# Delta rule with unscaled q and k: norms moved into gate tables, u and the output norm; triangle blocks loaded in pieces

## What is computed

```
q = jnp.repeat(l2_norm(q), rep, axis=2) * DN_HEAD_DIM ** -0.5     # l2_norm(x) = x * rsqrt(sum(x*x) + 1e-6)
k = jnp.repeat(l2_norm(k), rep, axis=2)
g = -exp(a_log) * softplus(a + dt_bias);  beta = sigmoid(b);  gc = cumsum(g) in the chunk
m = where(strict, beta * (k k^T) * decay, 0) + eye                 # decay = exp(gc_i - gc_j)
u0, w = triangular_solve(m, [v * beta, k * beta * exp(gc)])
u = u0 - w @ state;  o = q_dec @ state + (q k^T * decay) @ u;  state = cd * state + k_dec^T @ u
o = rms_norm(o, out_g)
```

## Time and profile before

| | |
|---|---|
| median of 3 runs | 3026.83 us (3018.61 to 3031.2) |
| the profiled execution, and its span | 3026.03 us, 3024.1 us |
| PE busy | 2846.4 us (94%) |
| DVE, ACT, POOL busy | 1903.4 us (63%), 1408.8 us (47%), 362.9 us (12%) |
| mean granted PE clock | 0.975 |

### The profile page before, as it was taken

One profiled execution on the slowest core, in us unless ns is written; L12 is line 12 of the kernel. 1 busy time (PEld: TensorE's weight loads), 2 busy tenths in 40 slices (PEclk: granted clock), 3 DMA queues, 4 the chain that ended last, 5 costly groups with the idle time before them and its releaser, 6 DMA issues.

```text
span 3024.1 us, 46453 instructions
## 1 busy us (share of the span) xinstructions
PE 2846.4 (94%) x19394; PEld 2681.0 (89%) x19394; DVE 1903.4 (63%) x2801; ACT 1408.8 (47%) x2399; POOL 362.9 (12%) x338
## 2 busy tenths in 40 slices
PE   6999998798999999999989999998999999999996
PEld 6999998687888999999988999998887899988775
DVE  5546647642333544656456855776888888878886
ACT  5346544355555433443335204433555555545554
POOL 0000010011112000002200002222122111112210
PEclk9999999899999999999999999999999999999998
DMA  4444435422232554444434458998999988889984
GB/s 185 169 157 145 171 103 178 150 98 73 78 100 94 204 181 169 167 168 158 157 127 156 152 203 312 371 362 325 366 361 363 357 326 317 324 333 345 357 338 142
DMA packets 112048, 668.47 MB, mean 221 GB/s; under 512 B 28336, under 2 KB 28552, under 8 KB 33920
## 3 DMA queue, kind: packets, MB, share of 16 engines
q1 hardware_dynamic: 86976, 496.93, 45.4%
q0 software_dynamic: 23712, 164.11, 14.8%
q10 hardware_dynamic: 1152, 4.47, 0.4%
HBM read 651.54 MB, written 13.30 MB: 220 GB/s over the span
## 4 chain that ended last, share of the span: by engine, by line
PE 66%; DVE 13%; DMA 10%; ACT 7%; issue 2%; SPq 0%; POOL 0%; DVEq 0%; ACTq 0%
PE PS L1001 66%; DMA raw<-in_pv 8%; DVE WL L1626 5%; DVE m L1617 3%; ACT WH L2304 3%; ACT m L2289 2%; DMA m<-in_pv,keep 1%; DVE m L2129 1%; ACT L2289 1%; DVE m L1817 1%; DMA raw<-in_w_kv 1%; DVE m L1814 0%; ACT m L2290 0%; PE PS L1004 0%; DVE m_896r L2222 0%
## 5 line engine op out<-in xcount | busy, mean ns | idle before, releaser
L1626 DVE TENSOR_TENSOR WL<-raw,WH 128x1024 fp32r<-128x1024 f32 x804 | 985.5, 1233 | 672.8 <-ACT WH L2304 671.9
L2304 ACT CAST WH<-raw 128x1024 fp32r<-128x1024 f32 x804 | 837.3, 1046 | 571.2 <-PE PS L1001 371.6
L1001 PE MATMUL PS<-m_4096r,WH 128*128 128x256 f32 x5184 | 997.9, 293 | 31.1 <-DVE m_4096r L1617 11.5
L1001 PEld LDWEIGHTS PS<-m_4096r,WH 128*128 128x128 f32 x5184 | 827.1, 196 | 54.7 <-issue 13.2
L1001 PE MATMUL PS<-m_4096r,WL 128*128 128x256 f32 x2592 | 743.5, 287 | 0.0
L1001 PE MATMUL PS<-m_8192r,WH 128*128 128x256 f32 (+1 forms) x2560 | 561.1, 313 | 16.7 <-issue 11.1
L1001 PE MATMUL PS<-WH,m_896r 128*128 128x512 f32 x1536 | 524.1, 394 | 24.6 <-DVE m_896r L2222 24.5
L1001 PEld LDWEIGHTS PS<-m_4096r,WL 128*128 128x128 f32 x2592 | 507.1, 196 | 0.0
L1001 PEld LDWEIGHTS PS<-m_8192r,WH 128*128 128x128 f32 x2560 | 398.6, 194 | 19.6 <-issue 11.7
L1001 PE MATMUL PS<-m_8192r,WL 128*128 128x192 f32 (+1 forms) x1792 | 405.1, 273 | 0.0
L1001 PE MATMUL PS<-WL,m_896r 128*128 128x512 f32 x1024 | 401.5, 392 | 0.0
(11 more groups left out here) (228 smaller groups left out, 1869.7 us busy)
## 6 DMA issues: line engine op xcount, KB each, us to landing
raw<-in_pu SPq DMA_DIRECT2D x128, 1024.0 KB, 6.9
raw<-in_pv SPq DMA_DIRECT2D x128, 1024.0 KB, 8.7
raw<-in_w_qkv SPq DMA_DIRECT2D x48, 1024.0 KB, 4.8
raw<-in_w_o SPq DMA_DIRECT2D x48, 1024.0 KB, 4.8
raw<-in_w SPq DMA_DIRECT2D x40, 1024.0 KB, 4.8
raw<-in_w_z SPq DMA_DIRECT2D x32, 1024.0 KB, 4.9
raw<-in_w_kv SPq DMA_DIRECT2D x16, 1024.0 KB, 4.8
raw<-in_w_q SPq DMA_DIRECT2D x16, 1024.0 KB, 4.8
```

The lines of the kernel that those rows point to most:

```text
L1001: return e.matmul(o, l, x, start=start, stop=stop)
L1626: tt(WL[:, k, :], raw[:, n % NRAW, h * 1024:h * 1024 + 1024], WH[:, k, :].bitcast(F), ALU.subtract).then_inc(S["lo"], 1)
L2304: e.copy(WH[:, k, :], raw[:, n % NRAW, h * 1024:h * 1024 + 1024]).then_inc(S["hi"], 1)
```

## The change

Q and k stay as they come from the Silu. Of their norms, `RNK` = 1/|k| for 24 columns goes into two gate tables (beta for the inverse's table `BEN`, and the table `BX` that scales k into kb), into the rows of the stored k products (`iv_product`, now on DVE, line 1788 of the new kernel), and into u (`dn_u_`, ACT with a column of RNK as scale). The norm of q goes into the eps of the output norm, `EPSQ`, for which DVE gets an instruction of its own (`ysc`) between PE's sums and the Sqrt. The 12 `rn_spread` steps are gone, with the three parts after each. `iv_turn` now waits for DVE's `rn`. After `iv_out` stand 28 parts where 16 stood. The loads are in pieces with semaphores of their own: the block between (`im`) is stored and loaded after the third scaling; U is stored before the turning copy and T after it; POOL issues the loads of the first two groups. SP loads T and the block between of group g+2 once `X` of group g is done, and gates and U once `o3` is.

```
-        for n in range(12):
-            self.do("rn_spread", n)
-            yield
         st["n"] = True
...
         self.do("iv_out")
-        for g in range(2):
-            self.do("dn_load", g)
-        yield 16
+        yield 28
...
         self.do("dn_uc", g)
+        if g < 10:
+            self.do("dn_load_t", g + 2)
...
         self.do("dn_y", g)
         if g < 10:
-            self.do("dn_load", g + 2)
+            self.do("dn_load_u", g + 2)
...  SyncE
+            def dn_load_t(g):
+                s.wait_ge(*at(f"dn_pe{g % 2}", dn_at(DN_PE, g - 2, "X")))
+                for c in range(2):
+                    load_t(e, g, c)
+                    load_bt(e, g, c)
+            def dn_load_u(g):
+                s.wait_ge(*at(f"dn_pe{g % 2}", dn_at(DN_PE, g - 2, "o3")))
+                load_gates(e, g)
+                for c in range(2):
+                    load_u(e, g, c)
...  TensorE
             def iv_turn():
-                p.wait_ge(*at("keep", 1))
-                p.wait_ge(*at("rn_root", 1))
-                tr(PS[0:48, 2, 0:128], KEEP[:, 192:240])
-                tr(PS[0:48, 2, 128:256], KEEP[:, 48:96]).then_inc(S["iv_turn"], 1)
+                p.wait_ge(*at("rn", 1))
+                tr(PS[0:48, 2, 0:128], GC)
+                tr(PS[0:48, 2, 128:256], BEN).then_inc(S["iv_turn"], 1)
...  dn_in
-                p.wait_ge(*at(f"ld_dn{g % 2}", 176 * (g // 2 + 1)))
+                p.wait_ge(*at(t_sem(g), 96 * max(g // 2, 1)))
...  dn_uc
+                p.wait_ge(*at(u_sem(g), 80 * max(g // 2, 1)))
...  VectorE
             def rn_root():
                 v.wait_ge(*at("rn_root", 1))
-                v.step(recip(RN, RN))
+                ts(EPSQ, PS[:, 2, 0:24], 1e-6, 128e-6, ALU.add, ALU.mult)
+                v.step(recip(RNK, RNK))
                 v.own()
-                one(RN[:, 0:24], RN[:, 0:24], 128.0 ** -0.5, ALU.mult).then_inc(S["rn"], 1)
+                v.step(tt(by_head(BEN), by_head(BE), per_group(RNK), ALU.mult))
+                v.own()
+                tt(by_head(BX), by_head(BX), per_group(RNK), ALU.mult).then_inc(S["rn"], 1)
-            def rn_spread(n):
-                c = (n + 6) % 12
-                q = QK[:, c * 512:c * 512 + 512]
-                v.wait_ge(*at("rn_spread", n + 1))
-                v.wait_ge(*at("silu", 24))
-                tt(q, q, PS[:, 2 + (n + 1) % 6, :], ALU.mult).then_inc(S["qkn"], 1)
+            def iv_product(c):
+                v.wait_ge(*at("iv_product", c + 1))
+                for h in range(2):
+                    rows = slice(64 * h, 64 * h + 64)
+                    o = IV_STG[rows, 256 * c:256 * c + 256].rearrange("p (i k) -> p i k", i=4)
+                    scale = RNK[rows, 4 * c:4 * c + 4].unsqueeze(2).broadcast_to([64, 4, 64])
+                    tt(o, c4(PS[rows, 2 + (c + 1) % 6, :])[:, :, rows], scale, ALU.mult).then_inc(S["iv_kept"], 1)
             def dn_yss(g):
+                need_p(g, "yss")
+                mark(g, "ysc", stt(rr.rearrange("p (h t) -> p h t", h=2),
+                                   PS[:, dn_bank(g)[0], 0:4].rearrange("p (h t) -> p h t", h=2), 1.0 / 128, eps, ALU.mult,
+                                   ALU.add))
                 need_a(g, "yrt")
...  ScalarE
             def dn_u_(g, n):
-                mark(g, f"ut{n}", e.copy(dn_u(g)[b:b + 64, :], PS[b:b + 64, dn_bank(g)[0], 0:256]))
+                mark(g, f"ut{n}", act(dn_u(g)[b:b + 64, :], PS[b:b + 64, dn_bank(g)[0], 0:256], ACT.Copy,
+                                      scale=RNK[b:b + 64, 2 * g + t:2 * g + t + 1]))
             def dn_yss(g):
-                need_p(g, "yss")
-                mark(g, "yrt", act(dn_s(g)[:, 0:4], PS[:, dn_bank(g)[0], 0:4], ACT.Sqrt, scale=1.0 / 128, bias=C("eps6")))
+                need_v(g, "ysc")
+                mark(g, "yrt", act(dn_s(g)[:, 0:4], dn_s(g)[:, 0:4], ACT.Sqrt))
...  GpSimd
+            def iv_save(name, x):
+                for h in range(2):
+                    e.dma_start(by_chunk(scratch[name], h), x[48 * h:48 * h + 48, :]).then_inc(S[f"st_{name}"], 16)
+            def iv_scale(b):
+                if b < 2:
+                    return
+                g_.wait_ge(*at("iv_between", 1))
+                iv_save("im", IV_E[:, 2048:3072])
+                g_.wait_ge(*at("st_im", 32))
+                g_.wait_ge(*at("iv_zero", 6))
+                for g in range(2):
+                    for c in range(2):
+                        load_bt(e, g, c)
             def iv_out():
+                g_.wait_ge(*at("iv_inverse", 1))
+                iv_save("iu", IV_U)
                 g_.wait_ge(*at("iv_done", 1))
+                iv_save("it", IV_T)
+                g_.wait_ge(*at("st_iu", 32))
+                for g in range(2):
+                    for c in range(2):
+                        load_u(e, g, c)
+                    g_.wait_ge(*at("st_it", 32))
+                    for c in range(2):
+                        load_t(e, g, c)
+                    load_gates(e, g)
```

More of the change, by code:

```diff
@@ L122 @@
 DN_PE = ("X", "A", "C", "UC", "W", "u0", "s0", "u1", "o1", "s1", "u2", "o2", "s2", "u3", "o3", "yss", "ybc")
[L123 removed]
+DN_V = ("d1", "qk", "S0", "S1", "S2", "ysc", "yrc", "yn")
 DN_A = ("x", "eT", "eB", "k", "v0", "v1", "un", "nw", "ut0", "ut1", "ut2", "ut3", "y", "yrt")
@@ L754, in build @@
         KEEP, CDK = keep[:, 0:256], keep[:, 256:352]
-        GG, BE, KD, BX, GC = (KEEP[:, 48 * i:48 * i + 48] for i in range(5))
+        BE, KD, BX, GC = (KEEP[:, 48 * i:48 * i + 48] for i in range(1, 5))
         def sm(i):
@@ L992, in end @@
                     s.wait_ge(*at(f"raw{n % NRAW}", 16 * (n // NRAW + 1)))
-            Plan({"loads": loads, "mm": unit_mm, "vm": vm, "dn_load": dn_load, "end": end}).run()
+            Plan({"loads": loads, "mm": unit_mm, "vm": vm, "dn_load_t": dn_load_t, "dn_load_u": dn_load_u, "end": end}).run()
         def tensor_program(e):
@@ L1709, in sg_post @@
                 v.wait_ge(*at("sg_g", 1))
-                copy(KEEP[:, 0:48], sm(5))
                 copy(KEEP[:, 48:96], sm(6))
@@ L1800, in iv_scale @@
                 v.own()
-                v.step(tt(x, x, iv_spread(IV_BE[:, c:c + 32], 1), ALU.mult))
+                t = tt(x, x, iv_spread(IV_BE[:, c:c + 32], 1), ALU.mult)
+                if b == 2:
+                    t.then_inc(S["iv_between"], 1)
+                else:
+                    v.step(t)
             def iv_step(j):
@@ L2412, in rn_root @@
                 a.wait_ge(*at("ca_value", 8))
-                act(RN, PS[:, 2, 0:48], ACT.Sqrt, bias=C("eps6")).then_inc(S["rn_root"], 1)
+                a.wait_ge(*at("keep", 1))
+                act(RNK, PS[:, 2, 24:48], ACT.Sqrt, bias=C("eps6")).then_inc(S["rn_root"], 1)
             def mark(g, name, ins):
@@ L2433, in iv_turn @@
                 e.copy(IV_GB, PS[0:48, 2, 0:256]).then_inc(S["iv_gates"], 1)
-            def iv_product(c):
-                a.wait_ge(*at("iv_product", c + 1))
-                for h in range(2):
-                    rows = slice(64 * h, 64 * h + 64)
-                    o = IV_STG[rows, 256 * c:256 * c + 256].rearrange("p (i k) -> p i k", i=4)
-                    e.copy(o, c4(PS[rows, 2 + (c + 1) % 6, :])[:, :, rows]).then_inc(S["iv_kept"], 1)
             def iv_decay(b):
```

100 lines of the change are left out of this document (49 added, 51 removed).

## The result

The changed kernel takes 3006.18 us (median of 20 runs, 2993.9 to 3015.05), the kernel before on the same chip 3026.12 us (3012.31 to 3034.2). The ratio is 0.9934, with a 95% interval of 0.9921 to 0.9948: 20 us faster. The forecast was 3001, its range 2988 to 3017. The profiled execution took 3011.83 us, 5.7 above its median, with a span of 3010.0 us.

A forecast was written before the change was run, and what follows sets the result against it. PE, busy 94% of the span, was taken to bound the kernel, so only its queue and waits count. Terms -9.6 +2 -2.5 -14.8 -3 -1.3 +1.5 +3 = -24.7 took 3026.0 to 3001 us, range 2988 to 3017.

The forecast's parts named there:

- Spreads, decays, elimination: Transposes to turning copy: twelve spreads leave PE's queue (-9.6), waits behind the decays grow (+2), PE idles less in elimination (-2.5).
- rival 2: Early part: ACT is the limit and PE waits two full times around the decays; +10 over forecast, 3011; chance 0.10.
- First wait: Before the first group: PE's wait of 14.8 us for the stored triangles' loads goes; -14.8, at worst -3.
- Rival 1: First group: POOL's load chain is late, PE waits 10.7 us and the slow clock stays; +13.7, 3015; chance 0.14.
- The rule set beside it: U's stores: DVE's turning copy locks POOL out of writing DMA descriptors; first wait 0 to 1 us; left out of sum.
- Clock: Behind the first group's wait: without PE's rest the halved clock comes back; -3, bounds 0 and -4.5.
- u's scale: Groups: 48 ACT copies of u, 0.09 us longer each with a scale; +1.5, bounds 0 and +4.3.
- The groups: First group to output projection: the terms there, with the clock, come to +0.2.
- The wait for L2474: First group: PE's 2.5 us wait, behind a weight SP issued late, shrinks; -1.3, bounds -2.5 and +5.
- ysc: Output norm: an added DVE instruction before ACT's Sqrt; +3 together with shifted parts and value tiles, bounds -8 and +12.
- rival 3: Slower: ysc chains DVE and ACT in all twelve groups, PE waits 5.1 us in each; 3042 to 3048; chance 0.05.
- rival 5: It moves little: Rival 1 and rival 2 together, or late stored pieces and groups costing +12; 3018; chance 0.06.

The follow-up runs named there:

- the second trace: The changed kernel itself, unaltered, run and profiled again on the chip of three follow-up runs: 3005.21 us, 0.9929 to the kernel before.
- The run with 16 parts: The changed kernel with 16 parts after the inverse for 28, nothing else: 3012.56 us, 0.9967 to the kernel before.
- the copy on ACT: The changed kernel with the inverse's turning copy on ScalarE (ACT), not VectorE (DVE), nothing else: 3009.61 us, 0.9942 to the kernel before.
- the norms' part alone: The changed kernel with the loads of before: 22 loads on SP, 16 parts after the inverse: 3030.63 us, 1.0018 to the kernel before.
- the loads' part: The kernel before with pieces, POOL's loads and 28 parts of the changed one, spreads and norms as before: 3012.63 us, 0.9951.
- the well-placed 0.9978: The norms' part alone, with 18 parts for 20 between the decays and the scalings: 3015.56 us, 0.9978 to the kernel before.

## Why the prediction was right, and where it was off

The mechanism was right: the spreads' time comes out of PE's queue, and the pieces and parts remove most of the wait for the first group. The forecast is 5 us under the median: the gain was priced at 24.7 us and is 20 by the medians, 18.0 and 14.3 in the stage of the two traces. All three stretches fell short of their price in both traces, so the number is not made by errors that cancel. That the medians gained 2 to 6 us more than the stages of these single executions is not explained, and as far as it helped the forecast it is luck. Each term stands as follows.

*Spreads, decays, elimination* (-9.6, +2, -2.5, together -10.1): -9.1 measured. The products came 31 us earlier (ACT's first copy 38.5 us after the transposes by the earlier trace rows, DVE's first at 406.22, 7.9 us after); the prediction had said 32. The transposes behind DVE's three more operations cost nothing: the last of them ended at 395.91, PE came at 398.35. PE's idle time in the elimination fell by 3.6 us for the 2.5 taken. But of the 8.1 before, one wait of 2.03 stood behind the copy's start, at 577.51, where PE would have waited for the triangles anyway; without it the fall is 1.6. The decays' waits, taken as 8.6, were 1.14 and 9.06, 10.2 in this execution and 13.1 in the second trace. The 8 parts (6 us) between the two waits do not cover the chain there, in which ACT's Relus and Exps and DVE's instructions wait for one another. Placing the decays apart did not clearly shorten it; freeing DVE of the fills took 3.3 us off the longest wait, where the decay had been slow. The second trace lies nearly half way to rival 2. What on ACT would shorten it was not tried.

*First wait* (-14.8): -14.0 (-11.9 in the second trace), with 3.6 us (5.75) left where none was expected. PE arrived at 13.5 us after the copy's start for the 16.3 predicted, and the data at 17.1 for 14.8. PE's share, 2.8 us, costs nothing: the 7.3 from which its arrival was worked out held the convolution's wait of 2.03, which is gone. The step that failed is the landing of T's loads. The earlier trace rows has 1.7 us as a median of 48 loads, 40 of them beside the groups, where the DMA engines were busy for 0.28 of the time, and 8 issued while SP sent no weights. I carried it to a time with weights of 1 MB under way and a share of 0.84. POOL had T's four loads out at 13.2, as predicted (13.1), and the first matmul came 3.9 us later, not 1.7; the median of the four is 3.6, of all eight 4.8. The run with 16 parts has 1.9 with less traffic beside them. Rival 1 had named the reason, the weights' loads going on, but priced it at 10.7. The stores met their times: T landed 11.0 us after the copy's start, for 10.7.

*The rule set beside it.* It held, as the copy on ACT shows, and my reading of the row against it (1.13 ns an element) was wrong. It gives a later U, though only the second store was held, as the first went out ahead of the copy. T's own store waits for the copy anyway, so the wait of 3.6 is not due to it, though 0 to 1 us had been its forecast.

*Clock* (-3): the slow clock behind the first wait is shorter, not gone: in the ten us from the first group's first matmul the granted clock is 0.72 before, 0.84 after and 0.77 in the second trace. In the ten behind the wait in `dn_u` it is 0.60 and 0.70, where it was 1.00 before. Nothing was gained: PE's busy time times the missing share of the clock, summed over the third stretch, is 14.9 us before and 16.6 after, 14.4 in the second trace (an estimate from stretches of 5 us). *u's scale* (+1.5) is too small to measure.

*The groups* (+0.2 with the clock): +5.2, the largest error (+3.6 in the second trace). PE's waits in that stretch rose from 39.2 to 43.7 us: the reciprocal's by 2.6, u's by 2.4, POOL's squares by 1.9, the others fell by 2.3 together. The wait for L2474 (now L2499) fell from 2.50 to 1.14, as predicted (-1.3). In u's sum one wait rose by 3.6, that of the first group's second u (1.13 to 4.73), and others fell. ACT in the changed kernel there (L2478 is the copy of X for the second group), then the same copy before:

```profile
577.01 0.47 ACT L2322 ACTIVATE m<-PS,vecs 128x256 f32<-128x256 f32 x1 [3.14 <-PE PS L1027]
...
580.86 0.58 ACT L2478 COPY m<-PS 128x512 f32<-128x512 f32 x1
```
```profile
612.73 0.58 ACT L2453 COPY m<-PS 128x512 f32<-128x512 f32 x1
```

PE had begun the second group's products at 574.10, and at 610.49 before, so ACT took them up after 6.8 us for 2.2: a value tile's scaled copy and Silu stand ahead, and ACT had to wait 3.14 us for that tile's product. The first group's u queues behind the second group's tile copies. The prediction had named such a shift, by 2 parts within a unit, and priced it at a part of +3.

*ysc* (part of +3): as predicted, and rival 3 is out. (In rival 5, rivals 1 and 2 together would give 3025, not the 3018 written there.) The reciprocal's waits are 20.1 us in 5, between the 15 and 25 given. DVE at one of them (L1632 128x4 is ysc):

```profile
631.88 0.16 DVE L1632 SCALAR_TENSOR_TENSOR m<-PS,vecs 128x4 f32<-128x4 f32 x1
637.79 0.18 DVE L1889 RECIPROCAL m<-m 128x4 f32<-128x4 f32 x1 [5.76 <-ACT m L2322]
```

ysc is over 5.7 us before the reciprocal can start; ACT is late, as the earlier trace rows had it.

*What the prediction did not see*: that the norms' part alone is worth nothing or 0.2%, by two parts. SP's 22 loads hold back one weight, and where ACT's split of it falls against the copy of X is set by the place within a unit of 8 parts. Before, it fell behind that copy and waited 1.3 us. Removing the spreads with their parts moved it to where it cost 24 us of ACT and some 15 of the path; the loads' part, with POOL issuing, removed the held weight. So the parts are not independent: 1.0018 and 0.9951 multiply to 0.9969, the whole is 0.9934. With the well-placed 0.9978 for the first they give 0.9929.

## What to carry to other kernels

Price a transfer by a row in which the same other traffic runs; a landing time from quieter DMA engines is a lower bound. Take a second trace before reading a term of 2 or 3 us: here the same kernel's two traces differ by 1.6 to 3.1 us in a stretch. When a queue stands (here SP behind stored pieces), look which engine, in its fixed order, next needs what is queued behind it, and what stands behind that instruction: a shift of two small steps decided between 0.2% slower and 0.2% faster. Before crediting work put over a wait, check that the work's own inputs are not behind that same wait.

## What was not expected of the hardware

A DVE copy of 96x2048 float32 at 1.13 ns an element held POOL's two DMA issues for 3.19 us instead of 1.11, to 0.11 us after its end. A two-input DVE operation of 96x1024 beside POOL's fills of 128x512 took 1.63 or 1.64 us in four of the traces and 4.48 to 4.56 in five, with the same order of instructions around it, and 1.21 in the two where the fills don't run beside it. In all four short cases POOL's first fill started 0.08 to 0.41 us ahead of it, and the six fills took 4.4 to 4.7 us; in all five long ones the fills started 0.01 to 0.10 behind it and took 3.4. PE's wait behind it was 9.05 or 9.06 us in the four and 11.9 to 12.0 in the five. So a start that moves by a tenth of a microsecond goes with 2.9 us of PE's time; why the engine that starts first is the one that takes longer is open. ACT needs 3.88 us for the copy that DVE does in 2.33.
